# Post norms of a 1024-wide two-block network: last tiles and next first tiles on TensorE by halves of the tokens

## The reference, cut to what matters

```
for i in range(2):
    m = diff_attention(rmsnorm(x, pre_mixer[i]))      # i == 0
    m = short_conv(rmsnorm(x, pre_mixer[i]))          # i == 1
    x = x + rmsnorm(m, post_mixer[i])
    m = square(relu(rmsnorm(x, pre_mlp[i]) @ w_up)) @ w_down
    x = x + rmsnorm(m, post_mlp[i])
```

## Time and profile before

| | |
|---|---|
| median of 3 runs | 2313.03 us (2312.94 to 2314.38) |
| profiled execution, its own time (span) | 2311.9 us, that is 1.1 below the median of the runs |
| TensorE busy | 2292.4 us, 99%, 10627 matmul passes |
| VectorE busy | 1282.6 us, 55% |
| ScalarE busy | 823.4 us, 36% |
| GpSimd busy | 96.5 us, 4% |
| DMA | 220.00 MB, 95 GB/s on average |

### The profile page before, as it was taken

One profiled execution on the slowest core, in us unless ns is written; L12 is line 12 of the kernel. 1 busy time (PEld: TensorE's weight loads), 2 busy tenths in 40 slices (PEclk: granted clock), 3 DMA queues, 4 the chain that ended last, 5 costly groups with the idle time before them and its releaser, 6 DMA issues.

```text
span 2311.9 us, 29028 instructions
## 1 busy us (share of the span) xinstructions
PE 2292.4 (99%) x10627; PEld 1841.2 (80%) x10627; DVE 1282.6 (55%) x1680; ACT 823.4 (36%) x1135; POOL 96.5 (4%) x82
## 2 busy tenths in 40 slices
PE   9999999999999999999999999999999999999999
PEld 8876888888865788888887777888887887888887
DVE  5453643444598654444547868554456755654453
ACT  5376532322423532322434555222224223322222
POOL 0000000000000000000004311000001001000002
PEclk9999999999999999999999999999999999999999
DMA  5210332332463233232332112323322332323321
GB/s 199 83 46 28 102 106 92 100 100 91 166 176 110 74 100 100 91 100 91 109 100 73 46 46 74 119 92 99 100 91 65 118 98 75 110 93 99 100 91 55
DMA packets 64793, 220.00 MB, mean 95 GB/s; under 512 B 8577, under 2 KB 8961, under 8 KB 64449
## 3 DMA queue, kind: packets, MB, share of 16 engines
q1 hardware_dynamic: 64704, 218.78, 30.1%
HBM read 208.56 MB, written 2.10 MB: 91 GB/s over the span
## 4 chain that ended last, share of the span: by engine, by line
PE 91%; DVE 4%; ACT 3%; issue 1%; DMA 0%; POOL 0%; DVEq 0%; SPq 0%; ACTq 0%; POOLq 0%
PE ps L1718 84%; PE ps L2160 2%; PE ps L2280 1%; DVE h L946 1%; PE ps L2254 1%; PE ps L2025 1%; ACT xh L470 0%; DVE xl L913 0%; PE ps L2040 0%; DVE spl L1100 0%; DVE acc L935 0%; DVE m L942 0%; PE ps L2270 0%; ACT ex L755 0%; ACT sph L589 0%
## 5 line engine op out<-in xcount | busy, mean ns | idle before, releaser
L1718 PE MATMUL ps<-xh,whi 128*128 128x512 f32 x1752 | 690.7, 394 | 0.2 <-DVE wlo L991 0.2
L1718 PE MATMUL ps<-xh,wlo 128*128 128x512 f32 x1752 | 682.4, 389 | 0.0
L1718 PE MATMUL ps<-xl,whi 128*128 128x512 f32 x1752 | 682.2, 389 | 0.0
L907 DVE TENSOR_TENSOR wlo<-raw,whi 128x1024 fp32r<-128x1024 f32 x380 | 473.3, 1246 | 230.0 <-ACT whi L386 220.7
L386 ACT ACTIVATE whi<-raw 128x1024 fp32r<-128x1024 f32 x380 | 398.7, 1051 | 479.8 <-PE ps L1718 478.4
L1718 PE MATMUL ps<-yh,whi 128*128 128x512 f32 x1116 | 437.0, 392 | 1.2 <-DVE m L1469 0.8
L1718 PE MATMUL ps<-yh,wlo 128*128 128x512 f32 x1116 | 434.5, 389 | 0.0
L1718 PE MATMUL ps<-yl,whi 128*128 128x512 f32 x1116 | 434.2, 389 | 0.0
L1718 PEld LDWEIGHTS ps<-xh,whi 128*128 128x128 f32 x1752 | 329.3, 188 | 76.8 <-issue 6.5
L1718 PEld LDWEIGHTS ps<-xl,whi 128*128 128x128 f32 x1752 | 329.2, 188 | 69.9 <-issue 3.1
L1718 PEld LDWEIGHTS ps<-xh,wlo 128*128 128x128 f32 x1752 | 329.0, 188 | 69.1
(11 more groups left out here) (281 smaller groups left out, 1863.1 us busy)
## 6 DMA issues: line engine op xcount, KB each, us to landing
raw<-stream SPq DMA_DIRECT2D x380, 512.0 KB, 3.5
u<-ub SPq DMA_DIRECT2D x118, 67.0 KB, 2.5
tapw<-taps SPq DMA_DIRECT2D x1, 3584.0 KB, 11.5
h<-x_t SPq DMA_DIRECT2D x8, 256.0 KB, 6.3
raw<-stream SPq DMA_DIRECT2D x8, 256.0 KB, 6.3
out_t<-h SPq DMA_DIRECT2D x8, 256.0 KB, 2.0
const<-consts SPq DMA_DIRECT2D x1, 1025.0 KB, 9.1
vec<-vecs SPq DMA_DIRECT2D x1, 180.0 KB, 8.8
```

The costliest lines, as they stand in the source:

```text
L907: dve.tensor_tensor(wlo[:, a.slot], raw[:, a.slot], whi[:, a.slot].bitcast(F32), ALU.subtract)\
L1718: mm = pe.matmul(out, lhs, rhs, start=first and n == 0, stop=last and n == 2, skip_group_check=skip)
```

## The change

1. `to_m` on TensorE: the first five (mlp1: four) of the eight tiles as before. The last three (mlp1: four) run first for tokens 0 to 255 (A) of each, then for tokens 256 to 511 (B) of each. Behind the B half of the first of them stands the sum of squares of half A (`post_sum`).
2. `split_round` takes the place of the filler matmuls and `first_round` at the two inner seams: half A of three tiles block by block, with the sum of squares of half B behind block 2; then half A of the fourth tile; then half B of all four, block by block for six blocks, then tile by tile; then the row sum, which now uses bank 3 instead of 7.
3. `post_split` on VectorE and the new `to_m` on ScalarE: norm, add, `xh` and `xl` in halves of 256 columns, all eight blocks of A and then all eight of B, with the evacuations of the last B halves and the splits of four weight tiles between them. On ScalarE squares 5, 6 and 7 of h now all stand behind the split of the next stage's first ring slot, and root B stands behind `xh` of block 3.
4. GpSimd adds the squares of the last tiles in halves.
5. The end: A halves are normalised by VectorE and added by GpSimd while TensorE works on the B halves of the last tiles; each half is written out by itself (16 writes of 256 columns instead of 8 of 512).
6. Some semaphores are shared (a few now stand for two events), and the banks of the first two rounds of mlp1 and sc are exchanged.

```diff
@@ scalar: to_m @@
+                def square_a(k):
+                    act.wait_ge(s("m_half"), sq0 + k - first + 1)
...
+                    act.activation(sq[:, k % 2, A_HALF], A["m"][:, k, A_HALF], ACT.Square).then_inc(s("sq_half"), 1)
...
+                for k in range(first, KB):
+                    square_a(k)
+                square_b(first)
+                root_a()
...
+                def x_a(k):
+                    act.wait_ge(h_added, NORM[which] - KB + k + 1)
+                    act.activation(xh[:, k, A_HALF], h[:, k, A_HALF], ACT.Copy, scale=col("pre", pre + k)).then_inc(xh_ready, 1)
...
+                split_hi(Tile(t0 + first))
+                x_a(0)
+                square_b(KB - 2)
+                split_hi(Tile(t0 + KB - 2))
+                x_a(1)
+                square_b(KB - 1)
+                split_hi(Tile(t0 + KB - 1))
+                x_a(2)
+                x_a(3)
+                root_b()
+                for k in range(4, KB):
+                    x_a(k)
                 for k in range(KB):
...
+                    x_b(k)
+                    if k >= LAG:
+                        square_block(following, k - LAG, h[:, k - LAG])
+                split_hi(Tile(tn))
+                for k in range(KB - LAG, KB):
+                    square_block(following, k, h[:, k])
@@ vector: post_split @@
+                for k in range(first, KB):
+                    sum_half(t0, k, which, A_HALF, add)
+                sum_half(t0, first, which, B_HALF, add)
+                norm_a(0)
+                add_a(0)
+                split_lo(Tile(t0 + first))
+                norm_a(1)
+                lo_a(0)
+                add_a(1)
+                sum_half(t0, KB - 2, which, B_HALF, add)
+                split_lo(Tile(t0 + KB - 2))
+                norm_a(2)
+                lo_a(1)
+                add_a(2)
+                sum_half(t0, KB - 1, which, B_HALF, add)
+                for k in range(3, KB):
+                    norm_a(k)
+                    lo_a(k - 1)
+                    add_a(k)
+                norm_b(0)
+                lo_a(KB - 1)
+                split_lo(Tile(t0 + KB - 1))
+                add_b(0)
+                for k in range(1, KB):
+                    norm_b(k)
+                    lo_b(k - 1)
+                    add_b(k)
+                    if k > LAG + 1:
+                        sq_sum(following, k - LAG - 1)
+                lo_b(KB - 1)
+                for k in range(KB - LAG - 1, KB):
+                    sq_sum(following, k)
@@ tensor @@
+            def split_round(t0, name, which):
+
+                base = X0[name]
+                for k in range(KB):
+                    pe.wait_ge(x_ready, base - KB + k + 1)
+                    for j in range(RING - 1):
+                        if k == 0:
+                            pe.wait_ge(wlo_ready, t0.plus(j).count)
+                        half_passes(t0.plus(j), RING + j, xh, xl, A_HALF, k)
+                    if k == 2:
+                        post_sum(which, B_HALF)
+                last = t0.plus(RING - 1)
+                pe.wait_ge(wlo_ready, last.count)
+                pe.wait_ge(ln_ready, SUM[which + "_post"] + 1)
+                for k in range(KB):
+                    half_passes(last, 2 * RING - 1, xh, xl, A_HALF, k)
+                for k in range(KB - 2):
+                    pe.wait_ge(x_ready, base + k + 1)
+                    for j in range(RING):
+                        half_passes(t0.plus(j), RING + j, xh, xl, B_HALF, k)
+                pe.wait_ge(x_ready, base + KB)
+                for j in range(RING):
+                    for k in range(KB - 2, KB):
+                        mm = half_passes(t0.plus(j), RING + j, xh, xl, B_HALF, k)
+                    mm.then_inc(tile_done, 1)
+                pe.wait_ge(evac_done, t0.count - 1)
+                row_sum(name, bank=3)
...
             def to_m(t0, which, y0):
-                down(Tile(t0), y0)
-                row_sum_halves(which)
+                first = KB - SPLIT[which]
+                for j in range(first):
+                    tile(Tile(t0 + j), j % RING, yh, yl, y_ready, y0)
+                for c in (A_HALF, B_HALF):
+                    for j in range(first, KB):
...
+                        for k in range(KB):
+                            mm = half_passes(t, t.slot, yh, yl, c, k)
+                        mm.then_inc(s("tile_half") if c is A_HALF else tile_done, 1)
+                        if c is B_HALF and j == first:
+                            post_sum(which, A_HALF)
+                if which == "mlp1":
+                    post_sum(which, B_HALF)
@@ sync: the output @@
             for k in range(KB):
+                sp.wait_ge(h_added_pool, k + 1)
+                sp.dma_start(out_t[k * P:(k + 1) * P, A_HALF], h[:, k, A_HALF]).then_inc(stored, 16)
```

More of the change, by code:

```diff
@@ L817, in to_m @@
             def to_m(t0, which):
-                for k in range(KB):
[L820 to L828, removed]
+                name, first, root = which + "_post", KB - SPLIT[which], LAST_ROOT if which == "mlp1" else rrow
@@ new lines, in root_b @@
+                def root_b():
+                    act.wait_ge(sum_ready, SUM[name] + 1)
+                    act.activation(lnb[:, B_HALF], ps[:, SUM_BANK, B_HALF], ACT.Ln, scale=1.0 / D, bias=EPS)\
+                       .then_inc(ln_ready, 1)
+                    act.wait_ge(ln_ready, SUM[name] + 1)
+                    act.activation(root[:, B_HALF], lnb[:, B_HALF], ACT.Exp, scale=-0.5).then_inc(rrow_ready, 1)
+                for k in range(first):
+                    act.wait_ge(evac_done, t0 + k + 1)
+                    square_block(name, k, A["m"][:, k])
+                    split_hi(Tile(t0 + k))
@@ L965, in post_norm, with sum_half @@
                     sq_sum(following, k)
[L967 to L972, removed]
-                dve.wait_ge(rrow_ready, SUM["mlp1_post"] + 1)
[L974 to L978, removed]
+            def sum_half(t0, k, which, c, add):
+                if c is A_HALF:
+                    dve.wait_ge(s("tile_half"), SPLIT_AT[which] + k - (KB - SPLIT[which]) + 1)
+                else:
+                    dve.wait_ge(tile_done, t0 + k + 1)
+                out, src, done = A["m"][:, k, c], ps[:, k % RING, c], s("m_half") if c is A_HALF else evac_done
+                if add:
+                    dve.tensor_tensor(out, src, out, ALU.add).then_inc(done, 1)
+                else:
+                    dve.tensor_copy(out, src).then_inc(done, 1)
@@ L1518, in add_to_m, with set_m @@
                 split_lo(t)
-            def set_m(t, k, halves=False):
+            def set_m(t, k):
                 dve.wait_ge(tile_done, t.count)
[L1522 to L1532, removed]
+                dve.tensor_copy(A["m"][:, k], ps[:, t.slot]).then_inc(evac_done, 1)
                 split_lo(t)
@@ L1867, in second_round, with post_sum @@
                         pe.wait_ge(ln_ready, SUM[name] + 1)
-                    tile(t.plus(j), RING + j, xh, xl, free=free)
+                    tile(t.plus(j), bank + j, xh, xl, free=free)
+            def post_sum(which, c):
+                name = which + "_post"
+                if c is A_HALF:
+                    pe.wait_ge(s("acc_half"), SPLIT_ADDS[which] + SPLIT[which] - 1)
+                else:
+                    pe.wait_ge(s("root_half"), 2 * POST[which] - 1)
+                    pe.wait_ge(acc_ready, ACC[name] + KB - 1)
+                pe.matmul(ps[:, SUM_BANK, c], cst("ones"), acc[:, c], start=True, stop=False)
+                if c is A_HALF:
+                    pe.wait_ge(s("sq_half"), SPLIT_AT[which] + SPLIT[which])
+                else:
+                    pe.wait_ge(sq_ready, SQ[name] + KB)
+                pe.matmul(ps[:, SUM_BANK, c], cst("ones"), sq[:, 1, c], start=False, stop=True)\
+                  .then_inc(s("sum_half") if c is A_HALF else sum_ready, 1)
@@ L2172, in _ @@
                     pe.wait_ge(s("piv_ready"), 1)
[L2173 removed]
+                    pe.matmul(ps[:, 7], cst("ones"), A["s1"][:], start=True, stop=True).then_inc(s("mean_mm"), 1)
                 if n >= 5 and n % 2:
```

258 lines of the change are left out of this document (196 added, 62 removed).

## The result

| | before | after |
|---|---|---|
| median | 2313.62 us of 5 runs (2312.94 to 2314.38) | 2331.30 us of 5 runs (2330.86 to 2333.35) |
| span of the profiled execution | 2311.9 us | 2331.6 us (its own time 2333.35) |
| TensorE busy, passes | 2292.4 us, 10627 | 2300.0 us, 11031 |

The ratio is 1.0079 [1.0068, 1.0090]: slower by 17.7 us, 6.1 above the forecast of 2325.2 and 0.3 above the top of its range. Every execution's time is 1.7 to 1.8 above its span, so the median one has a span of 2329.5; the profiled one is 2 longer, and its mean granted clock is 0.996 where the others have 0.997 or 0.998.

What follows compares the result with a forecast made beforehand. TensorE, busy 99% of the span, was taken to bound the kernel. 2311.9 us plus 14.4 for two seams, minus 2.2 at the end, gave 2324.1; plus 1.1, 2325.2 us, range 2318 to 2331.

Steps and rivals of the forecast that it cites:

- half of `xl`: VectorE's 256-column `xl` in a seam, not in the trace: taken as 0.48 us, like the norm's half.
- one turn in halves: Later blocks of a seam: add, `xh`, `xl` and handovers take 1.40 us a half block.
- wait at k = 0, 1, 2: TensorE's waits in a seam's A halves: 1.0 us for the third tile's weights, 0.3 for xl(1), 1.8 at xl(2).
- wait at k = 4: TensorE's wait in a seam's A halves for xl(4), as root B stands in front of xh(4): 0.9 us.
- wait at k = 5, 6, 7: TensorE's waits in a seam's A halves, eating a half block in 1.07 us against turns of 1.40: 0.24 each.
- row sum's wait: TensorE at a seam's end waits 3.6 us for sums of squares 5 to 7, behind the next tile's split.
- split start to row sum: Stretch of a seam from its first split tile to the row sum: 51.25 us.
- the end: Last tiles, norms and output of the kernel by halves: -2.2 us (-1.0 to -2.7).
- fillers removed: The seams' filler matmuls go: hidden in a wait, worth nothing themselves, 0 us.
- rival 1: Clock falls to half in the row-sum wait, a seam loses 2.3 us more: 2329.8 us, chance 0.12.
- x keeps up: TensorE stays the bound in the seams, 2 x -2.1 us, end -2.2: 2306.6 us, chance 0.05.
- The third: Chain of x hidden, row sum's wait stays: seam +1.5 us, end -2.2: 2313.8 us, chance 0.07.

Runs made afterwards that it cites:

- experiment 2: Kernel after, with squares 5 to 7 on ScalarE moved ahead of the split of the next weight tile: 2323.57 us.
- experiment 5: experiment 2's kernel, with VectorE computing the norm of block k + 1 ahead of `xl` of k - 1: 2319.62 us.
- experiment 6: Kernel after, same arithmetic in a new order on VectorE and ScalarE, norms and adds one to three blocks ahead of `xl`, sum B behind k = 1: 2310.60 us.
- experiment 3: Kernel before, without its six filler matmuls at each of three places (start of block two's first MLP, both seams): 2317.33 us.
- experiment 1: Kernel after, with fourteen filler matmuls that nobody reads in front of the row sum at both inner seams: 2327.61 us.

## Why the prediction was wrong by 6 us

| step | forecast | measured |
|---|---|---|
| half pass | 0.119 | 0.120 |
| half of `xl` | 0.48, bounds 0.37 to 0.75 | 0.48 to 0.49 |
| one turn in halves | 1.40 | 1.40 |
| wait at k = 0, 1, 2 | 1.0, 0.3, 1.8 | 0.78, 0.17, 1.66 |
| wait at k = 4 | 0.9 | 0.58, 0.77 |
| wait at k = 5, 6, 7 | 0.24 each | 0.22 each |
| row sum's wait | 3.6 | 3.73, 3.73 |
| split start to row sum | 51.25 | 51.64 (seam 2), 53.09 (seam 1) |
| the end | -2.2 | -1.8, -2.1 alone |
| clock behind the row sum's wait | full (chance 0.12 of half, 2.3 a seam) | half, 2.4 and 2.6 a seam |
| fillers removed | 0 | 3.6 for three places of the kernel before, as they held the clock |

**The direction and its mechanism held.** The serial chain of VectorE and ScalarE bounds the first part of a seam, the squares behind the next split bound its last, and both were where the prediction put them. Experiments 2, 5 and 6 take these terms away one by one, and the time follows. In experiment 2 the wait left was 1.95 where 2.1 was expected.

**The step that failed** is what the sum put on the passes behind the row sum's wait, nothing, and with it rival 1's chance of 0.12. Both were drawn from one row: "So 3.6 us of standing are seen at full clock, and not much more would be". One stand that ended well was read as what any stand would do. Here the clock fell 2.0 behind the last pass in seam 1 and 2.5 in seam 2, twice in two stands of 3.73, and around all three stands of 2.10 in the kernel without fillers; it did not fall in the two profiled stands of 1.95. The rows had a warning that was left unused: the six fillers before keep TensorE's stands to about 0.7, and they were priced at "nothing themselves". The rival's price came out close, 2.3 against 2.4 and 2.6; had it been the forecast, 2329.8 would have missed by 1.5. That is luck in part: no row gave the length of ten passes that the price assumes. The Trainium skill (TensorE: Matmul & The Clock Gate, Why this matters for your kernels) warns of idle gaps between bursts of matmuls, behind which the clock is at half. The trace agrees for these two waits (granted clock 0.53 and 0.56 in the windows over their second half), and the reading of the kernel's end against it was wrong.

**The range.** Its ends do not follow from the terms given with them: seams at +4.4 and the end at -2.7 make 2319.1, not 2318, and seams at +9.4 with the end at -1.5 make 2330.3, not 2331. The +4.4 also lies below the lowest seam, +5.7, that the prediction works out. At the top it has slow seams or the clock's fall, never both, and the run lies 0.3 above it with seams near the forecast and three falls. (The "sparse-coded stage" of its first paragraph is the short convolution.)

**The ledger** of the profiled spans, 2324.1 forecast and 2331.6 measured, 7.5 apart: the clock behind the row sums 5.0 (row sum to first pass 0.99 for 0.57, then 24 passes in 7.44 and 7.65 for 5.46), the fall at k = 2 of seam 1 1.45 (53.09 less 51.64), the two row sums, each 0.4 late apart from that, 0.8, the end 0.4, the earlier start -0.55, and 0.4 that is not followed up. To the median, 0.7 comes on top and 2 off. The time outside the span is 1.8, not the 1.1 that was taken from a median of three. And the other executions have less half clock than the profiled one: its 17 us take 0.0037 off the mean clock (0.996), 0.997 leaves room for 12 to 16 us and 0.998, which the median execution has, for 7 to 12. Which falls they lack, or which are shorter, no profile shows.

**The other rivals.** That x keeps up (2306.6) was rightly refused for this order of the work. It needed another order, and even experiment 6, which removes nearly all waits, gets to 2310.6. The third (2313.8) needed all waits ahead of the row sum to be misread; they were there.

## What to carry to other kernels

Splitting a tile in halves bought nothing by itself here: it shortens the first latency and doubles the number of handovers, so the instruction order of the engines that feed TensorE must get a lead of a block or more at the same time, and an instruction that waits for TensorE must stand behind all that TensorE waits for. Price a stand of the matmul engine twice, once for itself and once for the passes behind it at half clock (here every profiled stand of 2.10 us or more in a seam lost it, and none of 1.95 or less that stood alone, while waits of 0.78, 0.17 and 1.66 close together lost it twice in eight seams). A filler in a wait is not free to remove; look at the clock, not at the idle time, before pricing it at nothing.

## What the runs showed of the hardware

- The granted clock did not fall at a fixed delay: 2.0, 2.5 and 1.4 after the end of the last pass (the two row sums' waits of the kernel after, seam 1 of experiment 3), or 0.5 and 0.8 after TensorE had started again (k = 2 of the kernel after, seam 2 of experiment 3). The same waits of 0.78, 0.17 and 1.65 at k = 0 to 2 brought half clock in one seam of two in the kernel after and in experiment 1's, and in none of two in those of experiments 2 and 5.
- The stretches at half clock in the seven profiled falls lasted 3.4 (four) or 6.8 (three). In a seam one cost 1.1 (seam 2 of experiment 3) to 2.6.
- GpSimd's add on 256 columns took 0.74 in the kernel after, and 1.20 and 2.04 in experiment 6's, where it runs beside VectorE's 1024-column subtraction of a weight tile (1759.35 to 1760.58, 1764.70 to 1765.91). GpSimd's rows in experiment 6's timeline:

```profile
1759.97 1.20 POOL L1890 TENSOR_TENSOR acc<-acc,sq 128x256 f32<-128x256 f32 x1 [5.83 <-ACT sq L847]
1764.46 2.04 POOL L1890 TENSOR_TENSOR acc<-acc,sq 128x256 f32<-128x256 f32 x1 [3.28 <-ACT sq L847]
```

The subtraction itself took 1.21 to 1.23 there, as elsewhere. That it is the cause was not tried by itself.
